# First norm: where the modulation's scale is summed, and where its weights stand in the stream

## The chip, the cores and the metric

One core of a Trainium2 chip. The metric is the device time of one execution in microseconds (us). The kernel has TensorE (PE), VectorE (DVE), ScalarE (ACT) and GpSimd (POOL) with a queue of their own each, and SyncE (SP), which issues nearly all transfers. Everything is fp32 in memory; matmuls that matter are done in halves (see below).

## The reference, cut to what matters

Two layers of a transformer with adaptive norms, then two layers of other mixers (of no concern here). The part that the change touches is the very first norm:

```
c_act = jax.nn.silu(c)                                     # c: (1, 1024)
for l in range(2):
    mod = c_act @ w_ada[l] + b_ada[l]                      # 9 segments of 1024
    sh1, sc1, g1, sh2, sc2, g2, sh3, sc3, g3 = jnp.split(mod, 9, axis=-1)
    u = rms_norm(x) * (1 + sc1) + sh1                      # x: 256 positions x 1024
    x = x + 0.5 * g1 * ((silu(u @ w_gate) * (u @ w_up)) @ w_down)   # 1024 -> 2816 -> 1024
    ...                                                    # the attention part with sh2, sc2, g2
```

## The kernel before, in words

Activations are held transposed: 8 tiles (`KD`) of 128 features x 256 positions. All weights come as one stream of chunks of 512 KB (128 x 1024), in the order in which TensorE's program takes them (the list `order`); `RING` = 8 of them fit. SP issues chunk n when chunk n-8 has been used (L496). There are three kinds:

- "cut": a matmul weight. ACT copies its upper half (`weight_upper`, L2230), DVE subtracts to get the lower (`weight_lower`, L1520), and TensorE waits for the lower half. For each tile k there is a wide matmul (upper half with both halves of the activations, 512 columns) and a narrower one (lower half, 256 columns). The chunk's place is free when TensorE is done.
- "ada": one modulation chunk, the 128 outputs of a segment `seg` and tile k (number seg*8+k). DVE multiplies it with the activated `c`, laid out in rows (`c_rows`), and adds up along the row (L1531). Its place is free when DVE is done.
- "whole": TensorE reads it as it lies, in fp32 (`arrived`).

The engines do chunks ahead of need through `work_ahead`: every wait that goes through `due` first does the chunks that stand up to three cuts ahead. In the start (`starting`) that is off, and DVE does chunks where `modulated(...)` names them.

The start before the change: ACT squares the 8 tiles of x, TensorE sums the 8 squares over features with one-column matmuls (`squares_sum`, 16 matmuls), ACT and DVE take the root and its reciprocal, and `spread` broadcasts it by matmuls. `hold(b, n)` issues n matmuls of 128 columns into a bank that nobody reads. `spread(0)` ends with `hold(7, 60)`. DVE reduces 16 ada chunks in the order scale k, shift k (`ADA_FIRST`): seven before the norm's loop, nine in it (`normalise`). For each tile DVE scales, ACT adds the shift and rounds the upper half (`shift`), and DVE makes the lower half. Chunks 0 to 11 of the stream are ada, 12 to 14 are the three cuts of the first projections (gate 0, up 0, gate 1), 15 to 18 the last four ada, 19 and on the further projections. `project_wide_first` runs the three first projections tile by tile as the tiles come. In the feed-forward part, f counts the 22 pairs of gate and up; then `down` has 8 steps. 32 further ada chunks are taken in between by `ada_step`: four at f = 3, then about one for each of the remaining steps, nine of them in `down`.

Of the kernel before, what the change touches and what calls it, by code (L numbers as in the profile page):

```python
# [12 lines left out]
P = 128  # L13
# [87 lines left out]
def packed(parts):  # L101

    at, n = {}, 0
    for k, w in parts:
# [17 lines left out]
            ("b_in", 2 * KD), ("gate_b", 2 * KD), ("lam", KD), ("b_out", KD), ("mu", 6 * KD),  # L122
            ("w0", KD), ("a0", KD), ("k_k", KD), ("k_a", KD), ("r_k", KD), ("gn_g", KD), ("gn_b", KD)]
VEC_AT, VEC_W = packed(VEC_COLS)
# [90 lines left out]
def program(nc, dram, out, seen, stream):  # L215

    ctx = ExitStack()
    with ctx:
# [261 lines left out]
        ADA_STEPS = {0: KF + KD, 1: 18, 2: KF + KD, 3: KF + KD, 4: 18, 5: KF}  # L480
        ADA_FIRST = [seg * KD + k for k in range(KD) for seg in (1, 0)]
        slot_of = {}
# [6 lines left out]
        @block.sync  # L489
        def _(sp):  # L490
            led.taken = 0
            sp.dma_start(c_rows[:, :], dram["c_rows"]).then_inc(*did("c_in", 0, by=16))
            sp.dma_start(vecs[:, :], dram["vecs"]).then_inc(*did("vecs_in", 0, by=16))
            for n, (name, i, w) in enumerate(stream):
                if n >= RING:
                    sp.wait_ge(*of("weights_used", n - RING))  # L496
                sp.dma_start(ring[:, n % RING, 0:w], dram[name][i][:, 0:w]).then_inc(
                    led.sem(f"weights_in_{n % RING}"), 16)
            for j in range(KD // 2):
                sp.wait_ge(*of("x_added", ((DEPTH - 1, 5), 2 * j + 1)))  # L500
                sp.dma_start(out[:, 2 * j:2 * j + 2, :], X[:, 2 * j:2 * j + 2, :]).then_inc(
                    *did("out_stored", j, by=16))
            sp.wait_ge(*of("out_stored", KD // 2 - 1))
# [3 lines left out]
        def _(pe):  # L507
# [64 lines left out]
            def ada_step(s, step):  # L572

                n = ADA_STEPS.get(s, 0)
                if step < n:
                    chunks = [seg * KD + k for seg in ADA_AT[s] for k in range(KD)]
                    ada_take(chunks[len(chunks) * step // n:len(chunks) * (step + 1) // n])

# [23 lines left out]
            def spread(n):  # L602

                hold(7, 4)
                refill(4)
                pe.wait_ge(*of("rroot", n))
                for t in range(QT):
                    mn = mm(cols(4, P, t * P), root[:, 2, t:t + 1].broadcast_to((P, P)), ident, True, True)
                mn.then_inc(*did("rstd", n))
                readers[4] = [("rstd_read", n)]  # L610
                if n != "mem":
                    hold(7, 8 if n else 60)

# [59 lines left out]

            def project_wide_first(items, x, ready, after=()):

                for *_, b in items:
                    refill(b)
                took = [(*cut(name, i), done, readers_of, b) for name, i, done, readers_of, b in items]
                ada_take(after)
                for k in range(KD):  # L680
# [25 lines left out]
            def down(name, i0, x, kt, hidden, s, norm, reader="residual", ffn=None):  # L706
# [29 lines left out]
                else:  # L736
                    if norm == (1, 1):
                        mem_key(1, KD - 2, 7, 0, 4)
                    mix_sums(norm, 0 if norm == (1, 1) else 6)

            def ffn(s, l, which, norm, next_norm):
                spread(norm)
                def items(f):
                    return [(which + "_gate", l * KF + f, ("gate_raw", (s, f)), [("gate_up", (s, f))],
                             pair_bank(2 * f)),
                            (which + "_up", l * KF + f, ("up_raw", (s, f)), [("gate_up", (s, f))],
                             pair_bank(2 * f + 1))]

                project_wide_first(items(0) + items(1)[0:1], xn_hl, ("normed_lower", norm),
                                   ADA_FIRST[KD + 4:] if s == 0 else ())  # L750
                if s == 0:
                    hold(7, 8)
                else:
                    ada_step(s, 0)
                for f in range(1, KF):
                    if s or f > 3:
                        ada_step(s, f)
                    elif f == 3:
                        for step in range(f + 1):
                            ada_step(s, step)  # L760
                    for name, i, done, readers_of, b in items(f)[f == 1:]:
                        project_wide(name, i, xn_hl, done, readers_of, b)
# [275 lines left out]


            pe.wait_ge(*of("consts_in", 0))  # L1040
            for k in range(KD):
                squares_sum(0, k, KD)
            ada_take(ADA_FIRST[:KD + 4])
            for l in range(DEPTH):
# [460 lines left out]
        def _(dve):  # L1505
# [5 lines left out]
            def work_ahead(upto):  # L1511
# [3 lines left out]
                for n in range(worked[0], upto):  # L1515
# [7 lines left out]
                    elif kinds[n] == "ada":  # L1523
                        i = order[n][1]
                        half = 0.5 if i // KD % NMOD in (2, 8) else 1.0
                        if n == 0:
                            dve.wait_ge(*of("c_act", 0))
# [16 lines left out]
            def modulated(*chunks):  # L1544

                for i in chunks:
                    work_ahead(slot_of[i] + 1)
                    dve.wait_ge(*of("ada_mod", i))

            def lower(dst, k, src, upper, done, also=()):  # L1550
# [18 lines left out]
            def normalise(n, out_t, gain, event, ready=None):  # L1569
                dve.wait_ge(*due("rstd", n))  # L1570
                for k in range(KD + LAG):
                    if n == 0 and k < KD:
                        modulated(KD + k, k)
                    if k < KD:
# [167 lines left out]

            bias_steps()
            modulated(KD, 0, KD + 1, 1, KD + 2, 2)
            rstd(0)
            modulated(KD + 3, 3)
            lv = vec("lam", 0, KD)
# [467 lines left out]
        def _(act):  # L2215
# [56 lines left out]
            def shift(n, sh):  # L2272
                for k in range(KD):
                    if k == KD - 2:
                        starting[0] = False
                    act.wait_ge(*due("scaled", (n, k)))
# [139 lines left out]
            act.dma_start(X[:, :, :], dram["x"]).then_inc(*did("x_in", 0, by=16))  # L2416
            act.dma_start(consts[:, :], dram["consts"]).then_inc(*did("consts_in", 0, by=16))
            act.wait_ge(*due("c_in", 0))
            A.activation(c_rows[:, :], c_rows[:, :], ACT.Silu).then_inc(*did("c_act", 0))
# [7 lines left out]
            for l in range(DEPTH):  # L2427
                for s3 in range(3):
                    n = 3 * l + s3
                    shift(n, lambda k: mods(l, 3 * s3, k))  # L2430
                    if s3 == 1:
                        mix(l, n)
# [265 lines left out]
        def _(pool):  # L2698
# [22 lines left out]
            def added(n):  # L2721

                for k in range(n[1] != 5, KD):
                    pool.wait_ge(*of("mixed_n", (n, k)))
                    G.tensor_tensor(X[:, k, :], X[:, k, :], t_out[:, k, :], ALU.add).then_inc(
                        *did("x_added", (n, k)))

            for l in range(DEPTH):
                ffn(3 * l)
# [90 lines left out]
def laid_out(x):  # L2820
# [20 lines left out]
             "a_b_out_2", "b_mu_2", "b_w0_2", "b_a0_2", "b_k_k_2", "b_k_a_2", "b_r_k_2",  # L2841
             "b_gn_g_2", "b_gn_b_2"))], 1)
    d["w2"] = np.concatenate([np.stack([a[n][l] for l in L for n in ("cmpk_w2", "cmpv_w2")], 1)] * 2, 0)
    each = lambda f: np.concatenate([f(l) for l in L])
    d["w_ada"] = each(lambda l: a["w_ada"][l].T.reshape(-1, P, D))
    d["c_rows"] = np.repeat(a["c"], P, 0)
    for n in ("ffn1_gate", "ffn1_up", "ffn1_down", "ffn2_gate", "ffn2_up", "ffn2_down", "w_out"):
# [60 lines left out]
```

## Time and profile before

| | us |
|---|---|
| median of 3 runs | 2262.07 (2259.03 to 2268.75) |
| profiled execution, span from its first to its last instruction | 2258.5 |
| TensorE busy | 2177.8 (96%) |
| VectorE busy | 1526.8 (68%) |
| ScalarE busy | 1182.8 (52%) |
| GpSimd busy | 369.9 (16%) |

The profiled execution's own time is its span; the median of the timed runs stands 3.6 us above it. "Busy" leaves out waits. TensorE is busy nearly all the time, with matmuls that do nothing (`hold`) counted too.

### The profile page before, as it was taken

The numbers are of one execution on the slowest core, as the hardware profiler recorded it, in microseconds if no ns is written. First come the engines' busy times: TensorE is split into PE (matmuls) and PEld (weight loads), VectorE is DVE, ScalarE is ACT, GpSimd is POOL, SyncE is SP. The second block draws the span as 40 slices with busy tenths as digits, with TensorE's granted clock in tenths as the row PEclk, the third lists the DMA queues.
The fourth block names the chain that finished last, engine by engine and source line by source line (L and its number), as shares of the span: only waits on it lengthen the run. The fifth ranks groups of instructions, "written<-read, shape, count | busy, mean of one in ns | idle before, by whom it ended". The sixth has DMA issues, their size and how long they took to land.

```text
span 2258.5 us, 40704 instructions
## 1 busy us (share of the span) xinstructions
PE 2177.8 (96%) x16754; PEld 1932.4 (86%) x16754; DVE 1526.8 (68%) x2122; ACT 1182.8 (52%) x2059; POOL 369.9 (16%) x360
## 2 busy tenths in 40 slices
PE   7999999999999999999999999999999988999998
PEld 7888988988888889988888988788878978868887
DVE  6897767688778866767775874387557544626753
ACT  4554557565455544765554664365446431526542
POOL 0111022111102100311111103020232350303001
PEclk9999999999999999999999999999998999999999
DMA  7887662467768768434665443355524300434552
GB/s 277 328 308 252 242 244 94 149 236 259 243 232 295 274 214 315 161 103 165 214 223 186 166 159 130 131 170 186 177 91 150 103 4 12 160 129 146 190 186 95
DMA packets 114232, 417.79 MB, mean 185 GB/s; under 512 B 12672, under 2 KB 12928, under 8 KB 113664
## 3 DMA queue, kind: packets, MB, share of 16 engines
q1 hardware_dynamic: 113184, 410.34, 52.2%
q10 hardware_dynamic: 864, 4.84, 0.6%
q8 instruction: 134, 2.20, 0.4%
q14 instruction: 50, 0.41, 0.1%
HBM read 414.09 MB, written 1.05 MB: 184 GB/s over the span
## 4 chain that ended last, share of the span: by engine, by line
PE 81%; DVE 7%; ACT 5%; issue 4%; POOL 1%; DMA 1%; POOLq 0%; SPq 0%; DVEq 0%; ACTq 0%
PE banks L551 80%; DVE weight_lower L1520 1%; DVE weight_ring L1531 1%; POOL heap L2718 1%; ACT weight_upper L2230 1%; ACT xn_t L2354 1%; PE banks L954 1%; PE banks L1340 0%; DMA weight_ring<-w_ada_dram 0%; ACT L2264 0%; ACT xn_t L2277 0%; DMA weight_ring<-w_in_dram 0%; ACT heap L2387 0%; DMA weight_ring<-ffn_up_dram 0%; ACT xn_halves L2245 0%
## 5 line engine op out<-in xcount | busy, mean ns | idle before, releaser
L551 PE MATMUL banks<-xn_halves,weight_upper 128*128 128x512 f32 (+1 forms) x3680 | 1004.8, 344 | 11.3 <-DVE weight_lower L1520 8.1
L1520 DVE TENSOR_TENSOR weight_lower<-weight_ring,weight_upper 128x1024 fp32r<-128x1024 f32 x580 | 743.1, 1287 | 315.4 <-ACT weight_upper L2230 314.2
L551 PE MATMUL banks<-xn_halves,weight_lower 128*128 128x256 f32 x2832 | 802.0, 283 | 6.6 <-DVE xn_halves L1553 2.9
L2230 ACT ACTIVATE weight_upper<-weight_ring 128x1024 fp32r<-128x1024 f32 x580 | 607.9, 1054 | 351.7 <-PE banks L551 202.6
L551 PEld LDWEIGHTS banks<-xn_halves,weight_upper 128*128 128x128 f32 x3680 | 637.6, 190 | 99.5 <-issue 7.9
L551 PEld LDWEIGHTS banks<-xn_halves,weight_lower 128*128 128x128 f32 x2832 | 538.6, 190 | 9.9 <-DVE xn_halves L1553 3.2
L551 PE MATMUL banks<-hidden,weight_upper 128*128 128x512 f32 x1216 | 430.0, 397 | 0.0
L551 PE MATMUL banks<-hidden,weight_lower 128*128 128x256 f32 x1216 | 341.7, 281 | 0.0
L551 PEld LDWEIGHTS banks<-hidden,weight_upper 128*128 128x128 f32 x1216 | 228.6, 188 | 56.4
L2718 POOL TENSOR_TENSOR heap<-heap 128x256 f32<-128x256 f32 x120 | 122.0, 1021 | 930.5 <-ACT heap L2460 614.5
L551 PEld LDWEIGHTS banks<-hidden,weight_lower 128*128 128x128 f32 x1216 | 228.2, 188 | 0.0
L1531 DVE CUSTOM_DVE_ANT_0 weight_ring<-weight_ring,c_rows,vecs 128x1024 f32<-128x1024 f32 x144 | 185.5, 1292 | 27.6 <-DMA weight_ring<-w_ada_dram 27.2
L2707 POOL TENSOR_TENSOR heap<-heap 128x256 f32<-128x256 f32 x88 | 75.0, 853 | 498.4 <-ACT heap L2297 497.9
L551 PE MATMUL banks<-heap 64*64 64x64 f32 (+8 forms) x2432 | 121.8, 260 | 17.4 <-issue 6.7
L551 PEld LDWEIGHTS banks<-heap 64*64 64x64 f32 (+4 forms) x2432 | 104.6, 147 | 32.3 <-issue 23.0
L551 PE MATMUL banks<-heap,weight_ring 64*64 64x15 f32 (+2 forms) x944 | 111.0, 292 | 1.5 <-DVE heap L1995 0.7
L551 PEld LDWEIGHTS banks<-heap,weight_ring 64*64 64x64 f32 (+2 forms) x944 | 89.2, 161 | 17.9 <-issue 4.0
L2288 ACT ACTIVATE heap<-banks 128x512 f32<-128x512 f32 x88 | 52.2, 594 | 80.5 <-PE banks L551 80.5
L551 PE MATMUL banks<-consts 128*128 128x128 f32 x654 | 86.4, 284 | 0.0
L551 PEld LDWEIGHTS banks<-consts 128*128 128x128 f32 x654 | 79.9, 197 | 3.2 <-issue 2.7
L1599 DVE TENSOR_TENSOR heap<-banks,heap 128x512 f32<-128x512 f32 x88 | 60.5, 688 | 31.2 <-ACT heap L2288 30.3
L551 PE MATMUL banks<-consts,heap 64*64 64x64 f32 (+4 forms) x688 | 65.3, 248 | 14.0 <-ACT heap L2257 10.0
(299 smaller groups left out, 2496.1 us busy)
## 6 DMA issues: line engine op xcount, KB each, us to landing
weight_ring<-w_ada_dram SPq DMA_DIRECT2D x144, 512.0 KB, 4.5
weight_ring<-ffn_gate_dram SPq DMA_DIRECT2D x88, 512.0 KB, 3.8
weight_ring<-ffn_up_dram SPq DMA_DIRECT2D x88, 512.0 KB, 4.5
weight_ring<-ffn_down_dram SPq DMA_DIRECT2D x88, 512.0 KB, 3.4
weight_ring<-m_w_up_dram SPq DMA_DIRECT2D x64, 512.0 KB, 3.2
weight_ring<-m_w_down_dram SPq DMA_DIRECT2D x64, 512.0 KB, 3.2
weight_ring<-w_in_dram SPq DMA_DIRECT2D x58, 512.0 KB, 4.0
weight_ring<-b_w_rkv_dram SPq DMA_DIRECT2D x24, 512.0 KB, 3.2
```

Source lines behind the costliest of these rows:

```text
L551: return nc.tensor.matmul(o, w, r, start=first, stop=last)
L954: mn = nc.tensor.transpose(bank[0:n, 4 + j // 2, c:c + P], scores_of(u)[:, j, k * P:k * P + n], ident)
L1520: V.tensor_tensor(w_lo[:, n % RING, :], ring[:, n % RING, :], w_hi[:, j % SPLITS, :].bitcast(F32), ALU.subtract).then_inc(*did("weight_low ...
L1531: V.tensor_tensor_reduce(w, w, c_rows[:, :], half, vec("b_ada", i), ALU.mult, ALU.add, mod[:, i:i + 1]).then_inc(*did("ada_mod", i, also=[ ...
L1599: V.tensor_tensor(gu[:, f % 4], bank[:, b:b + 2, 0:S], gu[:, f % 4], ALU.add).then_inc(*did("gate_up", (s, f)))
L2230: A.activation(w_hi[:, j % SPLITS, :], ring[:, n % RING, :], ACT.Copy).then_inc(*did("weight_upper", j))
L2288: A.activation(gu[:, f % 4], bank[:, b:b + 2, S:2 * S], ACT.Copy).then_inc(*did("gate_up_half", (s, f)))
L2354: A.activation(s_, s_, ACT.Exp, bias=nmax[:, u % 4, j:j + 1], accum_out=den[:, u % 4, j:j + 1]).then_inc(*did("exp", (l, u, j), also=[("ex ...
L2707: G.tensor_tensor(gu[:, f % 4, 0, :], gu[:, f % 4, 0, :], gu[:, f % 4, 1, :], ALU.mult).then_inc(*did("hidden", (s, f)))
L2718: G.tensor_tensor(acc, acc, sum_tile(n, what, f), ALU.add).then_inc(*did("sum_added", (n, what, f)))
```

## The change

Eight chunks of the first layer's scale come in another layout (`w_scale`, as matmul weights), are read whole by TensorE, and are multiplied with `c` as a column (`scale_sums`: 8 fp32 matmuls with one column for each k); DVE only adds the bias to each result (`scale_mod`). The eight shift chunks stay with DVE. The squares of the first norm are added up by GpSimd first (`sums(0)`), as is done for the later norms, so TensorE sums two tiles and not eight. The 60 holds become 8 after the spread, 10 after each of the scale chunks 3 to 6, and 8 after the last. The three first cuts stand at places 13 to 15 of the stream and not 12 to 14. ACT cuts them when it comes to tile 5. The 32 further modulation chunks go one to each f from 6 to 21 and two to each of the 8 steps of `down`.

```diff
-        ADA_FIRST = [seg * KD + k for k in range(KD) for seg in (1, 0)]
+        ADA_FROM, CUTS_FROM = 6, 6
...
+            sp.dma_start(vecs[:, :], dram["vecs"]).then_inc(*did("vecs_in", 0, by=16))
             sp.dma_start(c_rows[:, :], dram["c_rows"]).then_inc(*did("c_in", 0, by=16))
-            sp.dma_start(vecs[:, :], dram["vecs"]).then_inc(*did("vecs_in", 0, by=16))
...
+                    if s == 0:
+                        up, each = KF - ADA_FROM, 2
+                        at = step - ADA_FROM if step < KF else up + each * (step - KF)
+                        if step >= ADA_FROM:
+                            ada_take(chunks[at:at + (1 if step < KF else each)])
+                        return
...
-                    hold(7, 8 if n else 60)
+                    hold(7, 8)
...
+            def scale_sums(k):
+
+                b = 3 if k % 2 else 6
+                refill(b)
+                w, used = arrived("w_scale", k)
+                for j in range(KD):
+                    mn = mm(bank[:, b, k:k + 1], w[:, j * P:(j + 1) * P], vec("c", j), j == 0, j == KD - 1)
+                mn.then_inc(*did("scale_raw", k, also=[used]))
+                readers[b] = [("scale_mod", k)]
...
+            def last_scales():
+
+                for k in range(CUTS_FROM, KD):
+                    ada_take([k])
+                    if k + 1 < KD:
+                        scale_sums(k + 1)
+                hold(7, 8)
...
                 spread(norm)
+                if s == 0:
+                    for k in range(3, CUTS_FROM + 1):
+                        scale_sums(k)
+                        if k < CUTS_FROM:
+                            ada_take([k])
+                        hold(7, 10)
...
                 project_wide_first(items(0) + items(1)[0:1], xn_hl, ("normed_lower", norm),
-                                   ADA_FIRST[KD + 4:] if s == 0 else ())
+                                   last_scales if s == 0 else None)
...
+            pe.wait_ge(*of("c_col", 0))
+            scale_sums(0)
+            ada_take([0])
             pe.wait_ge(*of("consts_in", 0))
-            for k in range(KD):
-                squares_sum(0, k, KD)
-            ada_take(ADA_FIRST[:KD + 4])
+            squares_of_two(0)
+            for k in range(1, 3):
+                scale_sums(k)
+                ada_take([k])
...
+            def scale_mod(k):
+
+                dve.wait_ge(*of("scale_raw", k))
+                V.tensor_tensor(mod[:, KD + k:KD + k + 1], bank[:, 3 if k % 2 else 6, k:k + 1], vec("b_ada", KD + k),
+                                ALU.add).then_inc(*did("scale_mod", k))
...
-                        modulated(KD + k, k)
+                        modulated(k)
+                        if k > 2:
+                            scale_mod(k)
...
-            modulated(KD, 0, KD + 1, 1, KD + 2, 2)
+            dve.wait_ge(*due("bias_half", 0))
+            modulated(0)
+            scale_mod(0)
             rstd(0)
-            modulated(KD + 3, 3)
+            for k in range(1, 3):
+                modulated(k)
+                scale_mod(k)
...
-                    if k == KD - 2:
-                        starting[0] = False
+                    if n == 0 and k == CUTS_FROM - 1:
+                        work_ahead(slot_of["cuts"])
...
+            act.wait_ge(*due("vecs_in", 0))
+            A.activation(vec("c", 0, KD), vec("c", 0, KD), ACT.Silu).then_inc(*did("c_col", 0))
...
+            sums(0)
```

## Rows read from the trace of the kernel before

**Rows 1.** The page: busy time, share of the span, instructions of each engine.
```profile
PE 2177.8 (96%) x16754; PEld 1932.4 (86%) x16754; DVE 1526.8 (68%) x2122; ACT 1182.8 (52%) x2059; POOL 369.9 (16%) x360
```

**Rows 2.** Stretches: us, busy us and count of each engine, granted clock, DMA share, GB/s.
```profile
0.00:50.00 50.00, 37.19 (x237) 35.26 (x238) 32.42 (x59) 20.75 (x37) 0.20 (x4) 1.00 0.70 266
50.00:100.00 50.00, 45.49 (x250) 39.17 (x249) 43.89 (x56) 28.53 (x43) 7.50 (x8) 0.97 0.86 310
100.00:150.00 50.00, 50.00 (x291) 44.10 (x290) 42.91 (x57) 28.18 (x45) 9.58 (x9) 1.00 0.91 341
185.00:230.00 45.00, 45.00 (x256) 39.10 (x256) 32.98 (x41) 18.84 (x22) 6.52 (x6) 1.00 0.71 250
```

**Rows 3.** The chain that ended last, in order of time: start, us, what.
```profile
1.64 7.81 DMA weight_ring<-w_ada_dram
...
9.63 1.15 DVE weight_ring L1531
...
46.48 6.47 DMA weight_ring<-ffn_up_dram
...
62.00 68.03 PE banks L551 x382
```

**Rows 4.** Timeline of TensorE, the start: start, us, engine, line, operation, count.
```profile
8.38 6.99 PE L551 MATMUL banks<-consts,heap 128*128 128x1 f32 x32 [8.38 <-ACT heap L2257]
...
17.92 1.19 PE L551 MATMUL banks<-consts,root 128*128 128x128 f32 x4 [0.64 <-DVE root L1567]
18.90 3.41 PE L551 MATMUL banks<-consts 128*128 128x128 f32 x15
```

**Rows 5.** Stretches of TensorE alone: us, busy us and count, granted clock, DMA share, GB/s.
```profile
14.00:15.00 1.00, 1.00 (x6) 1.00 1.02 410
21.00:22.00 1.00, 1.00 (x7) 1.00 1.04 414
23.00:24.00 1.00, 1.00 (x11) 1.00 1.02 410
64.00:64.50 0.50, 0.50 (x3) 0.50 1.02 377
269.00:270.00 1.00, 1.00 (x7) 0.50 0.46 184
```

**Rows 6.** Timeline of TensorE, later: one column, then 128 columns.
```profile
264.48 2.29 PE L551 MATMUL banks<-consts,heap 128*128 128x1 f32 x20
...
235.32 1.95 PE L551 MATMUL banks<-consts 128*128 128x128 f32 x16
```

**Rows 7.** Timeline of GpSimd: six additions of 128 x 256 in a row, twice.
```profile
1253.01 6.82 POOL L2718 TENSOR_TENSOR heap<-heap 128x256 f32<-128x256 f32 x6 [15.89 <-ACT heap L2681]
...
1375.38 8.45 POOL L2718 TENSOR_TENSOR heap<-heap 128x256 f32<-128x256 f32 x6 [1.24 <-ACT heap L2676]
```

**Rows 8.** Timeline of ScalarE and VectorE in the start.
```profile
7.63 2.54 ACT L2257 ACTIVATE heap<-x_t 128x256 f32<-128x256 f32 x8
8.14 0.19 DVE L1560 TENSOR_SCALAR vecs<-vecs 128x48 f32<-128x48 f32 x1 [8.14 <-DMA vecs<-vecs_dram]
...
41.14 1.28 DVE L1531 CUSTOM_DVE_ANT_0 weight_ring<-weight_ring,c_rows,vecs 128x1024 f32<-128x1024 f32 x1
...
20.33 0.17 DVE L1748 TENSOR_SCALAR lam<-vecs 128x8 f32<-128x8 f32 x1
...
33.02 3.50 DVE L1520 TENSOR_TENSOR weight_lower<-weight_ring,weight_upper 128x1024 fp32r<-128x1024 f32 x3 [1.64 <-ACT weight_upper L2230]
```

**Rows 9.** Timeline of TensorE from its first projection matmul to the third pair.
```profile
36.77 0.47 PE L551 MATMUL banks<-xn_halves,weight_upper 128*128 128x512 f32 x1 [2.67 <-DVE weight_lower L1520]
...
46.63 1.95 PE L551 MATMUL banks<-consts 128*128 128x128 f32 x16
...
55.35 0.50 PE L551 MATMUL banks<-xn_halves,weight_upper 128*128 128x512 f32 x1 [0.56 <-DVE weight_lower L1520]
...
62.00 0.47 PE L551 MATMUL banks<-xn_halves,weight_upper 128*128 128x512 f32 x1 [3.61 <-DVE weight_lower L1520]
```

**Rows 10.** Timeline of ScalarE: chunk gate 2 arrives; pairs 3 and 4 are read.
```profile
49.33 1.06 ACT L2230 ACTIVATE weight_upper<-weight_ring 128x1024 fp32r<-128x1024 f32 x1 [4.43 <-DMA weight_ring<-ffn_gate_dram]
...
69.41 0.60 ACT L2288 ACTIVATE heap<-banks 128x512 f32<-128x512 f32 x1 [0.46 <-PE banks L551]
...
74.95 0.60 ACT L2288 ACTIVATE heap<-banks 128x512 f32<-128x512 f32 x1 [0.95 <-PE banks L551]
```

**Rows 11.** Timeline of SP: gate 2 is issued.
```profile
46.11 0.33 SPq L497 DMA_DIRECT2D weight_ring<-ffn_gate_dram  x1
```

More of the change, by code:

```diff
@@ L122 @@
             ("b_in", 2 * KD), ("gate_b", 2 * KD), ("lam", KD), ("b_out", KD), ("mu", 6 * KD),
-            ("w0", KD), ("a0", KD), ("k_k", KD), ("k_a", KD), ("r_k", KD), ("gn_g", KD), ("gn_b", KD)]
+            ("w0", KD), ("a0", KD), ("k_k", KD), ("k_a", KD), ("r_k", KD), ("gn_g", KD), ("gn_b", KD), ("c", KD)]
 VEC_AT, VEC_W = packed(VEC_COLS)
@@ L672, in project_wide, with project_wide_first @@
                 readers[b] = readers_of
-            def project_wide_first(items, x, ready, after=()):
+            def scale_sums(k):
[6 more added lines that the diff above has]
+                readers[b] = [("scale_mod", k)]
+            def project_wide_first(items, x, ready, after=None):
                 for *_, b in items:
                     refill(b)
+                first = len(order)
                 took = [(*cut(name, i), done, readers_of, b) for name, i, done, readers_of, b in items]
-                ada_take(after)
+                if after:
+                    slot_of["cuts"] = first + len(items)
+                    after()
                 for k in range(KD):
@@ L749, in ffn @@
                 project_wide_first(items(0) + items(1)[0:1], xn_hl, ("normed_lower", norm),
-                                   ADA_FIRST[KD + 4:] if s == 0 else ())
[L751 to L754, printed above, removed]
-                for f in range(1, KF):
[L756 to L760, printed above, removed]
+                                   last_scales if s == 0 else None)
+                ada_step(s, 0)
+                for f in range(1, KF):
+                    ada_step(s, f)
                     for name, i, done, readers_of, b in items(f)[f == 1:]:
@@ L1525, in work_ahead @@
                         half = 0.5 if i // KD % NMOD in (2, 8) else 1.0
-                        if n == 0:
+                        if i == 0:
                             dve.wait_ge(*of("c_act", 0))
@@ L1548, in modulated @@
                     dve.wait_ge(*of("ada_mod", i))
+            def scale_mod(k):
+                dve.wait_ge(*of("scale_raw", k))
+                V.tensor_tensor(mod[:, KD + k:KD + k + 1], bank[:, 3 if k % 2 else 6, k:k + 1], vec("b_ada", KD + k),
+                                ALU.add).then_inc(*did("scale_mod", k))
+                dve.wait_ge(*of("scale_mod", k))
             def lower(dst, k, src, upper, done, also=()):
@@ L2430, in _ @@
                     shift(n, lambda k: mods(l, 3 * s3, k))
+                    starting[0] = False
                     if s3 == 1:
@@ L2841, in laid_out @@
              "a_b_out_2", "b_mu_2", "b_w0_2", "b_a0_2", "b_k_k_2", "b_k_a_2", "b_r_k_2",
-             "b_gn_g_2", "b_gn_b_2"))], 1)
+             "b_gn_g_2", "b_gn_b_2", "c"))], 1)
     d["w2"] = np.concatenate([np.stack([a[n][l] for l in L for n in ("cmpk_w2", "cmpv_w2")], 1)] * 2, 0)
@@ L2845, in laid_out @@
     d["w_ada"] = each(lambda l: a["w_ada"][l].T.reshape(-1, P, D))
+    d["w_scale"] = tiles(a["w_ada"][0][:, D:2 * D])
     d["c_rows"] = np.repeat(a["c"], P, 0)
```

## The prediction

> **What bounds the kernel now.** Read the page's busy times first: TensorE is busy for 96% of the span [rows 1]. Then read the stretches: from 100 us on, through the feed-forward part, TensorE is busy for all 50 of 50 us; its idle time lies in the first 62 us [rows 2]. The chain of waits says what held it there: the first chunk's landing at 9.45 us, then VectorE's reductions of modulation chunks, then a transfer that starts only at 46.5 us, and from 62.0 us on TensorE itself [rows 3]. So the change is worth what it moves the moment at which TensorE begins its unbroken work. I measure that at the end of gate and up of pair f = 3, which ScalarE starts to read at 69.41 us; a pair later it is 74.95, so a pair takes 5.54 us and one projection 2.77 [rows 10].
>
> How the 69.41 comes about: TensorE's first projection matmul starts at 36.77 and the first three projections end at 46.6 (the hold starts then) [rows 9]. From there it is 22.8 us: five projections (5 x 2.77 = 13.9), a hold, waits for lower halves, of which the last two are 0.56 and 3.61 us [rows 9], and a stretch in which the granted clock is 0.50, which is 1.2 and not 2.4 GHz [rows 5]. Pair 3 took 69.41 - 62.00 = 7.41 us and not 5.54: the low stretch costs 1.87.
>
> **The price of TensorE's small matmuls.** The change lets TensorE do one-column matmuls in fp32. The squares' sums are of this form: 16 calls gave 32 records. In the start they took 6.99 us, 0.218 each [rows 4]; later 20 of them took 2.29 us, 0.115 each [rows 6]. The 128-column holds took 3.41/15 = 0.227 at 19 to 22 us [rows 4] and 1.95/16 = 0.122 later [rows 6]. The ratio of nearly two is the clock's two levels. The granted clock's column shows 1.00 in the start all the same, but the counts of records per us, 6 to 7 up to 22 us and 11 after it, show the lower level [rows 5]. So one scale chunk (8 calls, 16 records) costs 3.5 us at the lower level and 1.83 at the upper; a hold of 10 (20 records) 4.5 or 2.4; a hold of 8, 3.6 or 1.95.
>
> Which level will there be? Before the change TensorE ran one-column matmuls from 8.38 to 15.4 us without a pause and stayed low; it rose only after the dense holds that began at 17.9 [rows 4, 5]. The other way round: 20 one-column records from 264.48 on, between dense matmuls, and at 269 the granted clock is 0.50, without any idle time [rows 5, 6]. One-column work neither lifts the clock nor keeps it up. The Trainium skill (TensorE: Matmul & The Clock Gate, Part 1: The HAM clock gate) says that sustained matmul activity releases the throttle, whatever the number of matmuls. By that rule TensorE would be at its upper level from the second scale chunk on; the rows above speak against it for matmuls of one column. What it would give is the third rival.
>
> **The change part by part, up to the spread.** The transfers are as many and as large as before (8 scale chunks for 8), so I let the first chunk land at 9.5 us as before [rows 3]. TensorE: scale 0 takes 3.5 us, to 13.0; then a hold of 3. The sums of two tiles need GpSimd's sixth addition. ScalarE's squares begin at 7.63 before [rows 8]; `c_rows` now stands behind `vecs`, so I put them 0.6 later, and the second square is there at about 9. Six additions in a row took 6.82 and 8.45 us [rows 7]: end at 15.8 to 17.4, I take 16.0, the lower as the start has little else on GpSimd. 4 matmuls, 8 records: 1.75, to 17.75. Before, TensorE was through with its squares at 15.4, so this edit loses some 2 us. The root and its reciprocal lie beside scale 1 and 2, which stand ahead of the spread in TensorE's program: 7.0 us, to 24.75. A hold of 4 (8 records, 1.8) and the spread (1.19 [rows 4]): the spread ends at 27.75. Before it was 17.92 + 1.19 = 19.1. Bounds: 22.2 with the upper level from 13 us on (third rival), 29.2 with the slower additions.
>
> **From the spread to the projections.** TensorE does scale 3 to 6 with a hold of 10 each, then scale 7 and a hold of 8. At the upper level: 4 x (1.83 + 2.4) + 1.83 + 1.95 = 20.7. At the lower: 4 x (3.5 + 4.5) + 3.5 + 3.6 = 39.1. The first pair starts low: 8.0. The rest is 16.5 or 31.1. A hold is dense and can lift the clock, the next one-column chunk can drop it again; I take the middle, 23.8. The three projections start at 27.75 + 8.0 + 23.8 = 59.55.
>
> VectorE is no longer the bound: 8 reductions of 1.28 go (10.2 us) and 8 additions on 8 columns or fewer at about 0.17 come, plus the semaphores [rows 8]. For each tile it has 1.28 + 0.17 + some 0.9, against 4.2 to 8.0 us of TensorE, whose scale it waits for. The three lower halves (3.50 us, [rows 8]) fit between scale 5 and the end of the hold after scale 6, as ScalarE cuts the chunks at tile 5. Their transfers wait for the places of shift 2, scale 3 and shift 3, which are all used by 4 us after the spread. What VectorE's wait in `scale_mod` blocks is its own next reduction, which is hidden by the same margin. All these I cost at nothing; if the cover went, TensorE would wait up to 3.5 us.
>
> **The projections.** The tiles are there, so 24 pairs of matmuls run without a pause: 3 x 2.77 = 8.3 us, plus half of the cost of a low stretch, 0.9: end at 68.75. The hold that stood behind them (1.7) stands ahead now, and no modulation chunk stands between up 1 and gate 6. Up 1 and gate 2 are in the ring by then; the next chunk is issued when the three end. Gate 2 was such a one: issued at 46.11, there at 49.33, cut 1.06 later, and its lower half 1.22 after that [rows 10, 11]: 5.6 us against the cover of two projections, 5.5. The chunk behind it was used 55.35 - 46.48 = 8.9 us after its issue [rows 3, 9] against a cover of 8.3. The long wait of 3.61 goes, as four reductions stood ahead of that cut. So five projections take 13.9 + 0.1 + 0.5 + 0.7 for restarts = 15.2, and pair 3 ends at 83.95. That is 14.5 us later than 69.41.
>
> **Later.** `down` gets 16 and not 9 modulation chunks: 7 x 1.28 = 9 us more for VectorE and 3.7 MB more in some 61 us. In its later stretch VectorE is busy for 33.0 of 45 us and DMA moves 250 GB/s [rows 2], against 410 when it is full [rows 5]. 73% + 15% = 88% and 310 GB/s: nothing for TensorE, or up to 4 us if VectorE's bursts collide. Taking four chunks out of f = 3 is in the 15.2 already.
>
> Sum: span 2258.5 + 14.5 = 2273.0. The median stands 3.6 above the span, so 2276.6.
>
> **The rivals.**
> 1. The clock rises in the hold after scale 3 and stays up: 27.75 + 8.0 + 16.5 + 8.3 + 15.2 = 75.75, so +6.3: 2268.4. For it: holds of 10 take more than half of each pair's time. Against: the drop at 269 came after only 2.29 us of one-column work [rows 5, 6], and a scale chunk is 1.83.
> 2. It stays low up to the projections: 27.75 + 39.1 + 8.3 + 1.9 + 15.2 = 92.25, +22.8: 2284.9. For it: each low one-column stretch is 3.5 us. Against: the 3.41 us of holds up to 22 us were followed by the upper level [rows 4, 5].
> 3. The other side: one-column work counts as activity, and the clock is up from the sums of the squares on: 16.0 + 0.9 for these, scale 1 and 2 in 3.7, hold 1.0, spread 0.6. The spread ends at 22.2, then 20.7 + 8.3 + 15.2 = 66.4, -3.0: 2259.1. It decides if the scale chunks cost 1.83 each before 20 us. Against: 6.99 us of such work at 0.218 [rows 4].
> 4. VectorE becomes the bound in `down`, on top of the forecast: up to +4, 2280.
> That the change doesn't take VectorE's work away can't be: it is eight reductions fewer.
>
> **How the numbers follow.** About 0.5% (11.3 us) is what a measurement can tell from no change. Forecast 45% (38 of it over 11.3, 7 under); rival 1: 28%, within; rival 2: 10%, slower; rival 3: 12% (8 within, 4 faster, if more than the clock is better there); rival 4: 5%, slower. That gives faster 4%, within 43%, slower 53%. The range reaches down into rival 1's lower side and up to rival 2: 2263 to 2285, leaving out rival 3 and half of rival 2.
>
> **What would show it.** Records of one-column matmuls on the ring at 0.22 us before the spread, and a mix of both in the pairs after it; the spread's end near 27.8; TensorE's first wide matmul near 59.6 and not 36.8; pair 3 read near 84; VectorE waiting for TensorE and not the reverse. The prediction is wrong if the first wide matmul starts before 50 us, or if the waits after it don't shrink to about 1 us, or if `down` shows idle TensorE.

## The result, and the profile after

| | before | changed |
|---|---|---|
| median, us (20 runs each) | 2262.71 (2255.16 to 2268.75) | 2268.22 (2262.6 to 2275.03) |
| profiled execution, span | 2258.5 | 2265.0 |
| ratio | 1 | 1.0024, 95% interval 1.0012 to 1.0035 |

The change makes the kernel slower by 5.5 us (interval 2.7 to 7.9). I forecast 14.5, and the range held the time. The direction was right, the size was not: it is near that of the first rival (+6.3).

The page's busy times and the stretches of the changed kernel:

```profile
PE 2188.5 (97%) x16840; PEld 1943.7 (86%) x16840; DVE 1518.6 (67%) x2114; ACT 1184.9 (52%) x2060; POOL 370.3 (16%) x366
```
```profile
0.00:50.00 50.00, 39.36 (x271) 39.01 (x272) 22.34 (x50) 20.26 (x37) 5.35 (x10) 1.00 0.70 262
50.00:100.00 50.00, 50.00 (x285) 43.33 (x284) 36.02 (x42) 27.10 (x40) 5.65 (x7) 1.00 0.67 241
100.00:150.00 50.00, 49.48 (x285) 43.00 (x284) 41.52 (x53) 28.70 (x45) 8.99 (x9) 1.00 0.86 319
```

Against [rows 2], VectorE has 10.1 us less work in the first 50 us, as foreseen, TensorE has no idle time from 50 to 100 us, and yet the kernel is slower. TensorE's timeline shows why (columns as in [rows 4]):

```profile
9.53 3.54 PE L551 MATMUL banks<-vecs,weight_ring 128*128 128x1 f32 x16 [9.53 <-DMA weight_ring<-w_scale_dram]
...
15.67 1.86 PE L551 MATMUL banks<-consts,heap 128*128 128x1 f32 x8 [1.11 <-POOL heap L2764]
17.40 6.97 PE L551 MATMUL banks<-vecs,weight_ring 128*128 128x1 f32 x32
24.23 2.05 PE L551 MATMUL banks<-consts 128*128 128x128 f32 x8
26.07 1.06 PE L551 MATMUL banks<-consts,root 128*128 128x128 f32 x4
26.93 2.84 PE L551 MATMUL banks<-consts 128*128 128x128 f32 x16
29.60 1.84 PE L551 MATMUL banks<-vecs,weight_ring 128*128 128x1 f32 x16
31.30 2.48 PE L551 MATMUL banks<-consts 128*128 128x128 f32 x20
33.62 1.84 PE L551 MATMUL banks<-vecs,weight_ring 128*128 128x1 f32 x16
...
47.38 2.03 PE L551 MATMUL banks<-consts 128*128 128x128 f32 x16
49.17 0.48 PE L551 MATMUL banks<-xn_halves,weight_upper 128*128 128x512 f32 x1
...
57.72 0.40 PE L551 MATMUL banks<-xn_halves,weight_upper 128*128 128x512 f32 x1
```

Scale 0 to 2 cost 3.4 to 3.5 us each, and the spread ends at 27.0 us, 8 us later than before: 2.2 us of that are there when the squares' sums end (17.4 for 15.2 us), and the rest comes with scale 1 and 2, which stand between them and the spread. From 29.6 on a scale chunk costs 1.7 us (from its start to the next one's start) and a hold of 10 costs 2.3. VectorE waits for TensorE's scale sums in this stretch, and not the reverse:

```profile
35.57 0.16 DVE L1583 TENSOR_TENSOR mod<-banks,vecs 128x1 f32<-128x1 f32 x1 [1.81 <-PE banks L551]
```

The first wide matmul comes at 49.17, where before it came at 36.77 [rows 9]. The prediction named a start before 50 us as a sign that it is wrong. The three projections end at 57.72, when the next one's first matmul starts (before, the hold started at 46.63, [rows 9]). SP's next issue comes when the first of the three is through, half a microsecond before that (before: 46.11, [rows 11]), and ScalarE's reads mark pairs 3, 4 and 21 (before, pairs 3 and 4: 69.41 and 74.95, [rows 10]):

```profile
57.22 0.33 SPq L497 DMA_DIRECT2D weight_ring<-ffn_up_dram  x1
```
```profile
72.06 0.60 ACT L2331 ACTIVATE heap<-banks 128x512 f32<-128x512 f32 x1 [1.71 <-PE banks L551]
77.71 0.60 ACT L2331 ACTIVATE heap<-banks 128x512 f32<-128x512 f32 x1 [1.71 <-PE banks L551]
...
173.41 0.60 ACT L2331 ACTIVATE heap<-banks 128x512 f32<-128x512 f32 x1 [0.67 <-PE banks L551]
```

The three projections end 11.1 us later, but pair 3 only 2.65 later: 14.8 us and not 23.3 lie between SP's issue and the read. By pair 21 the delay is 4.16 (before it is read at 169.25), and `down` adds nothing: 61.97 us from there to its end (235.4 us), 61.98 before (to 231.2 us). Of the 1.5 us between pair 3 and pair 21, 0.5 is one wait of TensorE at 112 us, and 0.5 is the pace of the first five pairs: 5.65 us each here, 5.55 before; the rest lies around that wait. The last section comes back to that.

### The profile page after: what moved, and what is told of

Read it like the earlier page. It is cut to its first block, busy times and chain, and to the rows that moved or that the text cites. A ratio compares the mean times of both kernels' runs of the same rounds, so it can differ in the third digit from the quotient of the medians.

```text
span 2265.0 us, 40885 instructions
## 1 busy us (share of the span) xinstructions
PE 2188.5 (97%) x16840; PEld 1943.7 (86%) x16840; DVE 1518.6 (67%) x2114; ACT 1184.9 (52%) x2060; POOL 370.3 (16%) x366
## 4 chain that ended last, share of the span: by engine, by line
PE 81%; DVE 6%; ACT 5%; issue 5%; POOL 2%; DMA 1%; POOLq 0%; DVEq 0%; SPq 0%; ACTq 0%
PE banks L551 80%; DVE weight_lower L1550 1%; POOL heap L2764 1%; ACT weight_upper L2273 1%; ACT xn_t L2397 1%; PE banks L1370 0%; DMA weight_ring<-ffn_gate_dram 0%; ACT heap L2397 0%; DVE nmax L1692 0%; ACT heap L2411 0%; ACT L2307 0%; DMA c_rows<-c_rows_dram 0%; ACT heap L2430 0%; PE banks L980 0%; ACT xn_t L2320 0%
## 5 line engine op out<-in xcount | busy, mean ns | idle before, releaser
L1561 DVE CUSTOM_DVE_ANT_0 weight_ring<-weight_ring,c_rows,vecs 128x1024 f32<-128x1024 f32 x136 | 176.1, 1301 | 34.7 <-DMA weight_ring<-w_ada_dram 34.2
L551 PEld LDWEIGHTS banks<-consts,heap 128*128 128x128 f32 (+1 forms) x664 | 59.3, 175 | 10.0 <-issue 3.5
```

What stands on the lines that cost most here:

```text
L551: return nc.tensor.matmul(o, w, r, start=first, stop=last)
L1561: V.tensor_tensor_reduce(w, w, c_rows[:, :], half, vec("b_ada", i), ALU.mult, ALU.add, mod[:, i:i + 1]).then_inc(*did("ada_mod", i, also=[ ...
```

## The experiments

Ratios are to the kernel before on the same chip. "Pair 3" is the start of ScalarE's read in the profile: 69.4 before, 72.1 changed.

| kernel | pair 3 | end of `down` | ratio (95%) |
|---|---|---|---|
| before | 69.4 | 231.2 | 1 |
| changed | 72.1 | 235.4 | 1.0024 (1.0012 to 1.0035) |
| changed, once more | 71.3 | 235.7 | 1.0026 (1.0008 to 1.0044) |
| before + new places only | 64.1 | 228.4 | 0.9985 (0.9966 to 1.0003) |
| the same, once more | 63.8 | 226.9 | 0.9970 (0.9951 to 0.9988) |
| changed + old places | 78.9 | 240.7 | 1.0074 (1.0051 to 1.0097) |
| changed, no hold after the spread | 72.4 | 236.2 | 1.0057 (1.0036 to 1.0078) |
| changed, short holds | 74.9 | 238.6 | 1.0083 (1.0061 to 1.0106) |
| changed, early holds | 73.5 | 236.5 | 1.0035 (1.0019 to 1.0051) |
| changed, tiles for holds | 77.3 | 239.4 | 1.0082 (1.0055 to 1.0109) |
| the last two together | 80.5 | 244.2 | 1.0055 (1.0034 to 1.0076) |
| before + new places, cuts later | 65.3 | 229.0 | 0.9992 (0.9970 to 1.0014) |
| half of the scale on TensorE | 62.0 | 223.8 | 0.9935 (0.9911 to 0.9959) |
| three tiles on TensorE | 62.8 | 224.6 | 0.9976 (0.9958 to 0.9994) |

The "end of `down`" is the start of TensorE's first holds behind it. The times of the whole spread more than the profiles' early parts. In five kernels (old places, no hold after the spread, short holds, tiles for holds, half of the scale) the ratio stands 7 to 11 us farther from before than the end of `down` does, more than the intervals allow, in parts that no edit touches. One thing that differs there is the clock's low stretches. The stretch from 1900 to 1950 us, before and changed (third number from the right: granted clock; the work in it is shifted by some 6 us):

```profile
1900.00:1950.00 50.00, 50.00 (x289) 0.97 0.35 116
```
```profile
1900.00:1950.00 50.00, 50.00 (x278) 0.90 0.30 95
```

The whole time goes with it: of 30 timed runs of the kernel before on one chip, the five with a mean granted clock of 0.984 took 2264.2 to 2269.2 us, and the five with 0.990 or more took 2252.6 to 2259.3. The six runs with short holds have a mean of 0.983, the runs of before beside them 0.988. So I judge by the early rows and take the ratios as the check. Why the late parts differ from kernel to kernel stays open, and so the times of the whole say less about the edits than pair 3 does.

**Before, the new places of the 32 chunks only.**

```diff
+                    if s == 0:
+                        up, each = KF - 6, 2
+                        at = step - 6 if step < KF else up + each * (step - KF)
+                        if step >= 6:
+                            ada_take(chunks[at:at + (1 if step < KF else each)])
+                        return
...
-                    if s or f > 3:
-                        ada_step(s, f)
-                    elif f == 3:
-                        for step in range(f + 1):
-                            ada_step(s, step)
+                    ada_step(s, f)
```

> The kernel before with only the new places of the 32 further chunks. If the four chunks at f = 3 cause the 3.61 us wait and the low stretch after it (1.87 us), both go: -4 to -5.5 us against before, with gate 3's wait reduced to about 0.5 us. Rival: the chunk's transfer is what comes last at gate 3 (ring places come free only at 46 us), then the wait shrinks by the four transfers at 1.28 us only in part: -1 to -2 us; or nothing, if down takes it back.

> The kernel before with only the new places of the 32 further chunks, once more, on the chip of the kernels sent with it. Theory: pair 3 read at 64.1 again (69.4 before), as the four reductions no longer stand ahead of gate 3; total -3 to -5 us against before. The first time the pairs ran at 5.65 us each (5.55 in the profile of before), which took back 2 us by pair 21; if the pace is set anew in each execution, this profile may show 5.55 and then pair 21 at 165 us or earlier.

```profile
64.10 0.60 ACT L2290 ACTIVATE heap<-banks 128x512 f32<-128x512 f32 x1 [1.70 <-PE banks L551]
```
```profile
63.82 0.60 ACT L2290 ACTIVATE heap<-banks 128x512 f32<-128x512 f32 x1 [1.40 <-PE banks L551]
```

Pair 3 comes 5.3 and 5.6 us earlier than before: the full price of the wait of 3.61 and the low stretch. The end of `down` keeps 2.8 and 4.3 of it. The rest went between pair 3 and pair 21 (99.8 us before, 102.7 and 101.1 here, mostly by the slower pace of the last section), and nothing in `down` (61.7 and 62.0 us). The timed gain of the second run is 0.30% (0.12 to 0.49); the first is on the edge. So this edit is good, and the change's parts pull against each other: -5.3 for the places of the 32 chunks and +8.0 (64.1 to 72.1) for all the rest, that is the scale on TensorE together with the squares on GpSimd, the holds and the places of the cuts. No run takes these apart.

**The changed kernel with the old places.**

> The changed kernel with the 32 further modulation chunks where they stood before (four at f = 3, then one a step, nine in down). Theory: where they stand is worth little; four reductions ahead of gate 3 on VectorE again, as in the 3.61 us wait of before. But the ring holds up 1 and gate 2 already, so a wait of 1 to 3 us at gate 3: total +1 to +3 us against the changed kernel. Rival: down with 16 chunks costs time (VectorE 97% busy in some stretches), then this kernel is 1 to 4 us faster than the changed one.

TensorE's one wait there, and VectorE's rows ahead of it:

```profile
71.61 0.76 PE L551 MATMUL banks<-xn_halves,weight_upper 128*128 128x512 f32 x1 [4.27 <-DVE weight_lower L1549]
```
```profile
64.71 1.27 DVE L1560 CUSTOM_DVE_ANT_0 weight_ring<-weight_ring,c_rows,vecs 128x1024 f32<-128x1024 f32 x1
...
68.33 1.28 DVE L1560 CUSTOM_DVE_ANT_0 weight_ring<-weight_ring,c_rows,vecs 128x1024 f32<-128x1024 f32 x1
...
70.23 1.22 DVE L1549 TENSOR_TENSOR weight_lower<-weight_ring,weight_upper 128x1024 fp32r<-128x1024 f32 x1 [0.62 <-ACT weight_upper L2272]
```

Four reductions in a row, then gate 3's lower half. The sign was right, my 1 to 3 us too small: pair 3 is 6.8 us later than in the changed kernel. Some 0.85 us of that were there at the first wide matmul (50.0 us), as the level rose later in the hold behind the spread. The other 5.9 are the idle time of 4.27 and a low stretch behind it, in which the first wide matmul takes 0.76 us (0.48 otherwise), as at 62 us before. The rival (that `down` costs) is refuted: `down` takes 62.0 us here too. The ratio is 11 us above that of the changed kernel, more than pair 3 explains.

**The changed kernel without the 8 holds behind the spread.**

```diff
-                if n != "mem":
+                if n != "mem" and n != 0:
                     hold(7, 8)
```

> The changed kernel without the 8 holds that follow the first spread. Theory A (these holds, 16 dense records that the prediction left out, gave the unbroken dense stretch of some 5 us after which the rows at 29.6 us came at 0.115): without them the dense stretch is the hold of 4 and the spread, some 3 us; scale 3 then runs at 0.22 a record, the hold of 10 after it at 0.22, and only then does the level rise. 16 records at low level saved (2.7 us), 16 + 20 records at low in place of high lost (1.7 + 2.1 us): first wide matmul at 50 to 51 us and not 49.1, total +1 to +2 us. Rival B (the level rises by itself some time after the start of TensorE's work, whatever it does): scale 3 starts at 27.0 and the rise still comes at about 29.3; first wide matmul at 48 us, total -1 to 0 us.

```profile
27.04 3.41 PE L551 MATMUL banks<-vecs,weight_ring 128*128 128x1 f32 x16
30.32 3.81 PE L551 MATMUL banks<-consts 128*128 128x128 f32 x20
33.96 1.84 PE L551 MATMUL banks<-vecs,weight_ring 128*128 128x1 f32 x16
```

Theory A: scale 3 at the low level, the rise inside the hold behind it. No rise by time alone. But the loss is smaller than I had it (first wide matmul at 50 to 51): it comes at 49.5, only 0.35 later, and pair 3 0.35 later. By the profile these holds pay for themselves and no more; the ratio, 7 us above that of the changed kernel, is one of those that the early rows don't explain.

**The changed kernel with holds of 4 between the scale chunks.** The edit is `hold(7, 10)` to `hold(7, 4)`.

> The changed kernel with the holds between scale 3 to 6 cut from 10 to 4. If one-column work doesn't keep the level (the prediction's reading of the rows at 264 us), 1.74 us of it against 0.9 us of dense work lets it fall: scale chunks at 3.5 us again; the first wide matmul comes at 48 to 54 us and the projections start low, total 0 to +5 us against the changed kernel. Rival: one-column work keeps the level once it is up; then 4 x 6 calls at 0.232 us = 5.6 us are saved, first wide matmul at 44 us (VectorE's tiles take 2.5 us each and may hold it to 45), total -4 to -5.5 us.

```profile
29.66 1.84 PE L551 MATMUL banks<-vecs,weight_ring 128*128 128x1 f32 x16
31.37 1.14 PE L551 MATMUL banks<-consts 128*128 128x128 f32 x8
32.34 1.84 PE L551 MATMUL banks<-vecs,weight_ring 128*128 128x1 f32 x16
34.05 1.14 PE L551 MATMUL banks<-consts 128*128 128x128 f32 x8
35.02 2.78 PE L551 MATMUL banks<-vecs,weight_ring 128*128 128x1 f32 x16
37.66 2.06 PE L551 MATMUL banks<-consts 128*128 128x128 f32 x8
39.51 3.41 PE L551 MATMUL banks<-vecs,weight_ring 128*128 128x1 f32 x16
```

The level falls in the third chunk and every saved hold is lost again: pair 3 is 2.8 us later than in the changed kernel, inside the 0 to 5 expected. The total is not: its ratio is 13 us above. So one-column work doesn't keep the level, as read in [rows 6]; what I misjudged is that 2.3 us of holds between the chunks are enough here.

**The changed kernel once more.**

> The changed kernel as it is, beside the same runs of before as the three kernels sent with it. Theory: +4 to +7 us against before, of which +2.7 at the end of pair 3 (69.4 before) and about +1.5 more by the end of the pairs, because the pairs up to f = 8 run at 5.65 us each and not at 5.55 until TensorE stops for the first time. Rival: the pace of a pair is set anew in each execution; then this profile may show 5.55 from pair 4 on, and the same program's end of pair 21 moves by up to 1.5 us against the first profile (173.4).

Pairs 3 and 4 here are read at:

```profile
71.31 0.60 ACT L2331 ACTIVATE heap<-banks 128x512 f32<-128x512 f32 x1 [1.57 <-PE banks L551]
76.86 0.60 ACT L2331 ACTIVATE heap<-banks 128x512 f32<-128x512 f32 x1 [1.65 <-PE banks L551]
```

5.55 us apart, 5.65 in the first profile of the same kernel: the pace is a matter of the execution.

**Early holds, to have TensorE at its upper level before the first chunk lands.**

```diff
+            hold_early(8)                      # vec("pe", 0, P) as both operands, after vecs_in
             pe.wait_ge(*of("c_col", 0))
             scale_sums(0)
...
-            squares_of_two(0)
-            for k in range(1, 3):
-                scale_sums(k)
-                ada_take([k])
+            hold(7, 7)
+            scale_sums(1)
+            ada_take([1])
+            squares_of_two(0)
+            scale_sums(2)
+            ada_take([2])
```

> The changed kernel with dense holds of 8 on columns of vecs from their landing (5.8 us) on, 7 holds between scale 0 and scale 1, and the squares' sums between scale 1 and 2. Theory (until the spread TensorE is the bound, at its lower level because it has one-column work only): with the level up by 9.5 to 13 us, scale 0 to 2 cost 1.74 each and not 3.41; the spread ends at 21 to 23 and not 27.0, the first wide matmul comes at 43 to 45 and not 49.1; total -4 to -6 us against the changed kernel. Rival A: the holds of 3.6 us don't lift the level or the scale chunks drop it: then 7 holds at low level are added (3.2 us) beside the wait for GpSimd: spread at 27 to 29, total 0 to +2 us. Rival B: the tiles after the spread then wait for the ring (scale 5 and 6, cuts) and the gain stops at 2 us.

```profile
5.88 3.78 PE L551 MATMUL banks<-vecs 128*128 128x128 f32 x16 [5.88 <-DMA vecs<-vecs_dram]
9.61 3.54 PE L551 MATMUL banks<-vecs,weight_ring 128*128 128x1 f32 x16
13.01 3.33 PE L551 MATMUL banks<-consts 128*128 128x128 f32 x14
16.14 3.41 PE L551 MATMUL banks<-vecs,weight_ring 128*128 128x1 f32 x16
```

A miss, as its rival A had it: neither 3.8 nor 3.3 us of dense holds lifted the level. The spread ends at 28.5, pair 3 comes 2.2 us later than in the changed kernel's runs beside it, and the median is the same (2268.5 and 2268.6 us).

**Tiles of the first projections in place of holds.** The cuts stand at places 11 to 13, `project_wide_first` calls back before tiles 3 and 5 for scale 6 and 7, and `last_scales` holds no more.

> The changed kernel with the three cuts at places 11 to 13 of the stream, and the projections' first tiles done between scale 5, 6 and 7 (three tiles, scale 6, two tiles, scale 7, three tiles) in place of the holds after scale 6 and 7. Theory: TensorE is the bound from the spread to the projections' end (57.2 us), so 10 + 8 holds of 4.2 us in all go away, plus nothing else: end of the three projections at 52 to 54, total -3 to -5 us against the changed kernel. Rival: VectorE's cuts and reductions (3.5 + 3 x 2.5 us after scale 5) become the bound, and TensorE waits for tiles 5 to 7: -1 to 0 us.

SP's issue of up 1 and TensorE's two waits:

```profile
55.47 0.33 SPq L497 DMA_DIRECT2D weight_ring<-ffn_up_dram  x1
```
```profile
51.25 0.80 PE L551 MATMUL banks<-xn_halves,weight_upper 128*128 128x512 f32 x1 [1.17 <-DVE xn_halves L1591]
61.84 0.77 PE L551 MATMUL banks<-xn_halves,weight_upper 128*128 128x512 f32 x1 [5.71 <-DVE weight_lower L1551]
```

The three projections end 1.8 us earlier than in the changed kernel (I expected 3 to 5), and then TensorE has nothing: with the cuts at 11 to 13, up 1 (place 19) needs gate 0's place in the ring, which comes free only when the projections end. That wait is 5.71. I had left it out. It shows what the later places of the cuts are worth in the change: with 13 to 15, up 1 and gate 2 are in the ring by then.

**Both.**

> e6 and e7 together. Theory: the gains add, -8 to -10 us against the changed kernel, that is 2 to 5 us faster than before the change. Rival: the ring or VectorE bounds after the spread, as e7's rival has it; -4 to -6 us against the changed kernel, within 1 us of before.

Pair 3 at 80.5, 8.4 us later than in the changed kernel: the two misses (1.5 and 5.3) add up and 1.7 us more come, with a wait at up 1 of 5.12 us. The forecast of a gain of 8 to 10 us was wrong. The median (2272.9) lies below that of the kernel with tiles alone (2282.0), against the early rows.

**Before, with the new places, the cuts at 14 to 16 and no hold behind the projections.**

> The kernel before with the new places of the 32 further chunks, the three first cuts at places 14 to 16 and not 12 to 14, and without the hold of 8 behind the three projections. Theory (the place of the cuts decides how many chunks behind them are in the ring while the three projections run: up 1 alone before, up 1, gate 2 and up 2 here): the wait of 0.7 us at gate 2 and the hold's 1.7 us go, the tiles come as late as before (43.3 and 44.4), the three projections end at 47 and pair 3 is read at 62 us (64.1 with the new places alone): total -1 to -2.5 us against that one, -4 to -6 against before. Rival: cuts behind tile 6's chunks delay the first matmul by 3 us and with it the end of the three projections to 49: 0 against the new places alone.

```profile
40.08 0.77 PE L551 MATMUL banks<-xn_halves,weight_upper 128*128 128x512 f32 x1 [6.48 <-DVE weight_lower L1519]
```

No wait remains between 40 and 100 us, but the first wide matmul comes 3.3 us later, after 6.48 idle and at the low level. Pair 3 is 1.2 us later than with the new places alone: the rival.

**Half of the scale on TensorE.** TensorE sums tiles 4 to 7, behind the spread; tiles 0 to 3 and the squares are as before.

```diff
+            for k in range(KD):
+                squares_sum(0, k, KD)
+            ada_take([seg * KD + k for k in range(PE_FROM) for seg in (1, 0)])     # PE_FROM = 4
...
-                    for k in range(3, CUTS_FROM + 1):
+                    for k in range(PE_FROM, CUTS_FROM + 1):
...
+                        if k < PE_FROM:
+                            modulated(KD + k, k)
+                        else:
+                            modulated(k)
+                            scale_mod(k)
```

> The changed kernel with TensorE summing the scale of tiles 4 to 7 only, behind the spread (VectorE does tiles 0 to 3 for scale and shift, as before), all eight tiles of squares on TensorE, c_rows first again, 12 holds behind the spread, 10, 10, 4 and 4 between. Theory (TensorE's one-column work is costly ahead of the spread, where it runs at 0.22 a record and delays the spread from 19 to 27 us; behind it TensorE had only holds to do): spread at 19, scale 4 to 7 in some 14 us at the upper level, the three projections end at 44 to 46, pair 3 is read at 59 to 61 (69.4 before, 72.1 in the changed kernel): total -8 to -10 us against before. Rival: one of the scale chunks meets the lower level, or VectorE's tile 7 comes last: pair 3 read at 62 to 65, -4 to -6 us.

```profile
18.40 1.20 PE L551 MATMUL banks<-consts,root 128*128 128x128 f32 x4 [0.61 <-DVE root L1601]
19.39 3.83 PE L551 MATMUL banks<-consts 128*128 128x128 f32 x24
23.06 1.84 PE L551 MATMUL banks<-vecs,weight_ring 128*128 128x1 f32 x16
...
32.80 1.14 PE L551 MATMUL banks<-consts 128*128 128x128 f32 x8
33.78 2.19 PE L551 MATMUL banks<-vecs,weight_ring 128*128 128x1 f32 x16
...
37.54 0.77 PE L551 MATMUL banks<-xn_halves,weight_upper 128*128 128x512 f32 x1
```

This version beats both kernels: 0.65% faster than before (0.41 to 0.89). The spread ends at 19.4, scale 4 to 6 run at 1.7 us in a stretch in which TensorE had 60 holds before, VectorE is spared four reductions, and the ring stands as in the change. Pair 3 is at 62.0 and not 59 to 61: after the hold of 4 the last scale chunk (2.19) and the projections (0.77) meet the low level, the rival's mechanism. The profile places 7.4 us of the gain before the end of `down`; its span is 10.2 shorter, the median 14.2, and what the rest is stays open. Against the new places alone, which this kernel contains, pair 3 gains 1.8 to 2.1 us; the later places of the cuts and fewer holds came with the four chunks, and no run takes them apart.

**Three tiles on TensorE.**

> As the kernel with half of the scale on TensorE, but only tiles 5 to 7, and 16 holds behind the spread. Theory: TensorE has 3 x 1.74 + 10 x 0.23 = 4 us less in its row than with four tiles less 4 holds more (1 to 1.8); VectorE has one reduction more (1.3 us). If TensorE bounds, the three projections end 2 us earlier than with four tiles; if VectorE bounds, 1.3 us later. Total within 2 us of that one either way.

```profile
34.01 3.54 PE L551 MATMUL banks<-vecs,weight_ring 128*128 128x1 f32 x16 [3.49 <-DVE weight_lower L1547]
```

TensorE waits 3.49 us for the cuts and falls to the low level, so the last scale chunk costs 3.5: VectorE bounds again. Pair 3 is 0.8 us later than with four tiles. I expected the totals within 2 us of each other; the medians are 8.7 us apart, of which the profiles show 0.8 by the end of `down`.

## Why the prediction was right in sign and wrong in size

The forecast for pair 3 was +14.5, measured +2.65. Of the 11.9 us between them, 9.6 lie between the spread and the projections.

- **Up to the spread: right.** Scale 0 at the low level (3.54 for 3.5), the wait for GpSimd (its six additions took 5.9, the sums began at 15.67 for 16.0), scale 1 and 2 in 6.97 for 7.0; the spread ends at 27.0 for 27.75. The 16.0 was partly luck: the additions began at 9.75 and not at about 9, and took 0.95 us less than the nearer of the two rows.
- **From the spread to the projections: this step failed.** I forecast 31.8 us (8.0 for the first pair at the low level, then 23.8, the middle of both levels); it took 22.2. Two causes. I left out the hold of 8 which `spread` itself issues. It costs 2.7 us, and inside it the level rises; without it the first scale chunk does run low and costs 3.41 (no hold after the spread). And I took the middle where all four pairs ran at the upper level: 4.02 us a pair, for which I had 8.0 for the first and 6.1 on the mean for the others. The evidence I argued from, the drop behind 2.3 us of one-column work, is real, but with scale chunks of 1.7 us and 2.3 us of dense work between them the level stayed up. With holds of 4 it fell.
- **The three projections:** 8.55 for 9.2 (49.17 to 57.72); no low stretch, so the 0.9 set in for it was not due.
- **The five projections after them: right.** 14.3 for 15.2, TensorE without idle time, the wait of 3.61 and its low stretch gone; the 1.3 set in for waits and restarts was not due. The two kernels with the places alone confirm it from the other side (-5.3, -5.6).
- **Later:** `down` costs nothing in the profile, as the sum had it; 1.5 us came between pair 3 and 21, which I did not foresee. With the old places in the changed kernel this stretch takes 99.8 us as before, and with half of the scale on TensorE too, there with the new places; in all three the pairs run at the quicker of the two paces of the last section.
- **The clock's rule.** One-column records stayed at 0.22 us from 9.5 to 24.2 us, so the third rival's 2259 did not happen, and in the early-holds kernel even dense holds of 3.8 us did not lift the level. The rule of the Trainium skill (TensorE: Matmul & The Clock Gate, Part 1: The HAM clock gate) that sustained activity releases the throttle does not hold for one-column matmuls here.

The first rival comes nearest to the mechanism that was measured, the upper level in all pairs behind the first, and I gave it 28% because the drop at 269 looked like its refutation. It too has the first pair at 8.0, where 4.02 was measured, and it too leaves out the hold of 2.7. That its 2268.4 is the measured median is luck: at pair 3 it has 75.75 and not 72.06, and 1.5 us of the difference came back later, the rest in parts that no row of mine accounts for.

## What to carry to other kernels

- Work moved to an "idle" engine lies on the path if the engine has to do it before the step that all others wait for: put it behind that step, where the engine has only holds, and move only as much as balances the two engines. With all eight chunks on TensorE pair 3 is 8 us later than with the new places alone, with four of them 2 us earlier (62.0 against 64.1 and 63.8); squares, holds and cuts moved along, so this is not the price of the chunks alone.
- In a ring, count which later chunks are already in it when a long holder of places ends. That, not the transfer's speed, decided the wait after the first projections, in both directions.
- A wait of TensorE can cost more than itself: with four reductions ahead of one cut, 4.3 us of idle time became 5.9.

## What the runs showed that I had not expected

- The same matmuls run at two paces, 5.55 and 5.65 us a pair (1.9%), at a granted clock of 1.00 in both. A pace lasts over many pairs. In the changed kernel it changed where TensorE had stopped (at 112 us, from 5.65 to 5.55), with early holds at 112 us too, from 5.55 to 5.65, but with no wait in the trace. It differs between two executions of one kernel (77.71 - 72.06 and 76.86 - 71.31), so it moves the time by 1 to 2 us for reasons that no edit made. What sets it stays open.
- The moment of the rise varies: the 16 records behind the spread took 2.84, 2.38, 2.87, 3.50 and 2.10 us in five profiles with the same start. By the counts of records per us the rise came between 27 and 31 us. Without those holds it came at about 33 us, inside a hold of 3.81 us, while in the early-holds kernel a dense stretch of 3.78 us had none. The length of the last dense stretch alone doesn't tell.
- Six additions in a row on GpSimd took 5.87 us here, less than the 6.82 and 8.45 of [rows 7], while VectorE was mostly idle.
